# A differential-attention stage with its steps in another order on all engines

## The reference, cut to what matters

```python
h = rms_norm(x, norm1_g)
proj = h @ w_in                      # q, k: 4 heads x 2 components x 64; v: 4 x 128; xp: 4 groups x 128; gates
q = rms_norm(q, q_norm_g); k = rms_norm(k, k_norm_g)        # each over 64 channels
s = where(causal, (q @ k.T) * 64 ** -0.5, NEG_BIG)          # for both components c of a head
p = softmax(s)
a = (p[:, :, 0] - lam * p[:, :, 1]) @ v
a = rms_norm(a, subln_g) * (1 - lam_init)
...                                  # pooling branch, gates, w_up_attn, w_up_pool, w_o
u = square(relu(rms_norm(x) @ w_mlp_in)); x = x + u @ w_mlp_out
```

## Time and profile before

| what | value |
|---|---|
| time, median of 3 runs | 1289.74 us (1288.73 to 1290.46) |
| the profiled execution | 1288.65 us, its span 1286.8 us |
| TensorE busy | 1242.7 us, 97%, 6249 matmuls |
| VectorE busy | 960.5 us, 75%, 1450 |
| ScalarE busy | 562.1 us, 44%, 989 |
| GpSimd busy | 140.5 us, 11%, 229 |
| DMA | 174.38 MB, 136 GB/s on average |

### The profile page before, as it was taken

How to read it: one execution, slowest core, us unless ns; L and a number is a source line. 1 busy time by engine, 2 the same in 40 slices (tenths; PEclk the granted TensorE clock), 3 DMA queues, 4 the chain that set the end, 5 groups by cost and what they waited for, 6 DMA issues and landing times. The chain is left out here.

```text
span 1286.8 us, 17813 instructions
## 1 busy us (share of the span) xinstructions
PE 1242.7 (97%) x6249; PEld 1040.2 (81%) x6249; DVE 960.5 (75%) x1450; ACT 562.1 (44%) x989; POOL 140.5 (11%) x229
## 2 busy tenths in 40 slices
PE   4999898989999999999999999999999999999998
PEld 4878787878888888888888888888888878888887
DVE  4557777777898669783577877777778898979864
ACT  4446665665554322331344554453453423333330
POOL 2122323232200004000000000000000000000035
PEclk9999999999999999999999999999999999999999
DMA  8230202030246464632222445345459735253323
GB/s 275 89 115 2 83 1 81 0 98 17 83 156 207 143 205 153 226 129 99 99 82 93 167 150 172 137 142 172 151 181 349 284 126 202 98 206 121 96 96 135
DMA packets 113466, 174.38 MB, mean 136 GB/s; under 512 B 5469, under 2 KB 59378, under 8 KB 112882
## 3 DMA queue, kind: packets, MB, share of 16 engines
q1 hardware_dynamic: 113394, 173.44, 39.6%
HBM read 120.99 MB, written 52.43 MB: 135 GB/s over the span
## 5 line engine op out<-in xcount | busy, mean ns | idle before, releaser
L2202 PE MATMUL bank<-o_hi,s_hi 128*128 128x512 f32 x448 | 174.4, 389 | 1.8 <-DVE s_lo L2055 1.8
L2202 PE MATMUL bank<-o_hi,s_lo 128*128 128x512 f32 x448 | 174.3, 389 | 0.0
L2202 PE MATMUL bank<-slot_hi,featT_hi 128*128 128x256 f32 (+1 forms) x320 | 102.8, 321 | 1.0 <-ACT qkv L959 1.0
L2111 DVE TENSOR_TENSOR c<-bank,c 128x512 f32<-128x512 f32 x112 | 75.6, 688 | 35.6 <-PE bank L2202 34.0
L2202 PE MATMUL bank<-featT_hi,pair_hi 128*128 128x512 f32 x256 | 99.8, 390 | 0.8 <-DVE c L2111 0.7
L2202 PEld LDWEIGHTS bank<-o_hi,s_hi 128*128 128x128 f32 x448 | 84.1, 188 | 19.8 <-DVE s_lo L2055 2.2
L2202 PE MATMUL bank<-featT_hi,pair_lo 128*128 128x512 f32 x256 | 99.6, 389 | 0.0
L2202 PE MATMUL bank<-featT_lo,pair_hi 128*128 128x512 f32 x256 | 99.6, 389 | 0.0
L2202 PE MATMUL bank<-o_lo,s_hi 128*128 128x512 f32 x256 | 99.6, 389 | 0.0
L2202 PEld LDWEIGHTS bank<-o_hi,s_lo 128*128 128x128 f32 x448 | 84.1, 188 | 17.2
L2202 PE MATMUL bank<-slot_hi,featT_lo 128*128 128x256 f32 (+1 forms) x320 | 97.0, 303 | 0.0
(11 more groups left out here) (258 smaller groups left out, 3243.2 us busy)
## 6 DMA issues: line engine op xcount, KB each, us to landing
s_raw<-u_store SPq DMA_DIRECT2D x28, 1024.0 KB, 5.6
pair_raw<-in_w_mlp_in SPq DMA_DIRECT2D x16, 1024.0 KB, 6.0
u_store<-s_tile SPq DMA_DIRECT2D x64, 256.0 KB, 2.2
o_raw<-in_w_mlp_out SPq DMA_DIRECT2D x16, 1024.0 KB, 8.3
u_store<-u_tile SPq DMA_DIRECT2D x48, 256.0 KB, 2.4
raw<-in_w_in SPq DMA_DIRECT2D x20, 512.0 KB, 7.0
gate_store<-out_tile SPq DMA_DIRECT2D x32, 256.0 KB, 2.1
gate_raw<-in_w_in SPq DMA_DIRECT2D x8, 1024.0 KB, 5.5
```

The costliest lines, as they stand in the source:

```text
L2111: nc.vector.tensor_tensor(out[:], psum, other[:], ALU.add).then_inc(up_sum, 1)
L2202: mm = nc.tensor.matmul(out, a, b, start=start and i == 0, stop=stop and i == len(steps) - 1)
```

## The change

- *First loads*: norm1_g is queued ahead of the first value weights. ScalarE rounds x block 0 one weight block earlier and squares x block 1 ahead of weight blocks 2 and 3; VectorE makes the rest of x block 0 one weight block earlier. TensorE transposes x block 1 in the middle of v_project(0), not ahead of it.
- *Order of the steps*: value products get lag 4 and the output lag 5, so the drain has 5 steps. TensorE's step is: half of the projection, scores, the other half, q/k transposes, transpose of attn_norm, [pool projection or project(h, 0)], value products, weight transposes to TB and to TA. The order on ScalarE, VectorE and GpSimd follows: VectorE begins with o_sum and the q/k normalisation, then w_tok, the weight rests, attn_norm, the two maxima, the q/k rests, take_attn, and the sum of squares last.
- *Mask*: two matmuls behind the scores, identity by mask, add the mask to the diagonal tile in the bank; VectorE's 64 additions are gone. Identity and mask are rounded once by ScalarE.
- *Drain*: late_weights(4) and keep_first(2) on ScalarE and c11_add(1) and side_add(4) on VectorE move from behind the drain into its step 3.

```diff
--- before.py
+++ after.py
...
+        ident_r = at("ident_r", 215, [P, P], F32R)
+        mask_r = at("mask_r", 215.5, [P, P], F32R)
...
-            return 4 if isinstance(h, int) and h == HEADS else T
+            return 5 if isinstance(h, int) and h == HEADS else T
...
             load_x(0)
+            sp.dma_start(g1_row[:], norm1_g.to_broadcast([P, D])).then_inc(g1_in, 16)
             load_v_w(0)
-            sp.dma_start(g1_row[:], norm1_g.to_broadcast([P, D])).then_inc(g1_in, 16)
             load_v_w(1)
             load_x(1)
...
-                    soft, ts, us, _ = lagged(h, s, 2)
-                    there, t, u, _ = lagged(h, s, 3)
-
-                    long_rows = soft and ts >= 3
-                    if soft and not long_rows:
-                        exponential(0, ts, us)
+                    there, t, u, _ = lagged(h, s, 4)
                     if there:
-                        act.wait_ge(tb_full, tb + 1)
+                        act.wait_ge(tb_full, tb)
...
+                    there, t, u, of = lagged(h, s, 5)
+                    if there and not (last and t == T - 1):
+                        take_attn(t, of, ta + 1)
+                        ta = ta + 1
+                    soft, ts, us, _ = lagged(h, s, 2)
+                    pools = s == POOL_STEP and s < steps(h)
+                    if soft:
+                        exponential(0, ts, us)
+                    if s == 0 and not first:
+                        take_projection(h, s)
+                        square_qk(h, s)
+                    if pools:
+                        if soft:
+                            exponential(1, ts, us)
+                        if first:
+                            act.wait_ge(h_ready, T)
+                        take_pool(BANK_USES * h + POOL_STEP + 2, GROUPS - 1 - h, 0)
                     if late:
                         late(s)
-                    there, t, u, _ = lagged(h, s, 3)
+                    there, t, u, _ = lagged(h, s, 4)
                     if there:
                         act.wait_ge(out_full, u + 1)
                         wait(act, out_free, u)
...
+                    if soft and not pools:
+                        exponential(1, ts, us)
...
             x_square(0)
             v_w_hi(0)
+            x_hi(0)
             v_w_hi(1)
-            x_hi(0)
+            x_square(1)
             v_w_hi(2)
             v_w_hi(3)
-            x_square(1)
             x_square(2)
+            act.wait_ge(const_ready, 2)
+            nc.scalar.activation(ident_r[:], ident[:], ACT.Copy)
+            nc.scalar.activation(mask_r[:], mask[:], ACT.Copy)
...
+                if s == 3:
+                    late_weights(4)
+                    keep_first(2)
             head(HEADS, middle, late, between)
-            late_weights(4)
-            keep_first(2)
...
-                            diagonal = bank[:, 2 * c + t // 4, t % 4 * P:(t % 4 + 1) * P]
-                            nc.vector.tensor_tensor(diagonal, diagonal, mask[:], ALU.add).then_inc(masked, 1)
-                            dve.wait_ge(masked, 2 * u + c + 1)
...
+                    there, t, u, _ = lagged(h, s, 5)
+                    if there:
+                        dve.wait_ge(out_part, u + 1)
+                        nc.vector.tensor_tensor(o_sum[t % 2][:], bank[:, OUT, 0:P], o_part[:], ALU.add).then_inc(out_free, 1)
+                    normalise_qk(h, s)
...
+                        if not first or t > 0:
+                            dve.wait_ge(tb_full, tb_uses)
+                            if t == 0 or t > 4:
+                                dve.wait_ge(ta_full, ta_uses)
                         nc.vector.scalar_tensor_tensor(w_tok[:, 0:n], prob[1][:, 0:n], coef, prob[0][:, 0:n],
                                                        ALU.mult, ALU.add).then_inc(w_tok_ready, 1)
-                    if s > 0 or first:
-                        sum_squares(h, s)
+                    there, t, u, _ = lagged(h, s, 4)
+                    if there:
+                        n = min(t + 1, 4)
...
+                    there, t, u, _ = lagged(h, s, 5)
+                    if there:
+                        dve.wait_ge(a_scaled, u + 1)
+                        nc.vector.tensor_scalar(attn_norm[t % 2][:], o_sum[t % 2][:], a_scale[t % 2], None,
+                                                ALU.mult).then_inc(a_normed, 1)
+                    there, t, u, _ = lagged(h, s, 2)
+                    for c in range(2):
+                        if there:
+                            n = (t + 1) * P
+                            dve.wait_ge(score_full, 2 * u + c + 1)
+                            nc.vector.tensor_reduce(neg_max[t % 2][:, c:c + 1],
+                                                    bank[:, 2 * c:2 * c + 2, :].rearrange("p a b -> p (a b)")[:, 0:n],
...
+                    tb_uses = tb_uses + lagged(h, s, 1)[0] + lagged(h, s, 3)[0]
+                    ta_uses = ta_uses + lagged(h, s, 5)[0] + (lagged(h, s, 3)[0] and lagged(h, s, 3)[1] >= 4)
+                    sum_squares(h, s)
+                    if middle:
+                        middle(s)
...
             x_norm(0)
             v_w_lo(0)
+            x_lo(0)
             v_w_lo(1)
-            x_lo(0)
             x_norm(1)
...
+                if s == 3:
+                    c11_add(1)
+                    side_add(4)
             head(HEADS, middle, between)
-            c11_add(1)
-            side_add(4)
...
+                            nc.tensor.matmul(bank[:, 2 * c + p0 // 512, 0:p1 - p0], a, b, start=i == 0,
+                                             stop=i == 2 and p1 < n)
+                for c in range(2):
+                    diagonal = bank[:, 2 * c + t // 4, t % 4 * P:(t % 4 + 1) * P]
+                    nc.tensor.matmul(diagonal, ident_r[:], mask_r[:], start=False, stop=True).then_inc(score_full, 1)
...
-                    second, third = (4, 4) if last and s > 0 else (3, 5)
-
-                    scores_first = projects and s in (1, POOL_STEP + 1)
-                    if scores_first:
-                        scores(h, s, tb)
-                    part(range(second))
-                    if not scores_first:
-                        scores(h, s, tb)
-                    there, t, u, _ = lagged(h, s, 3)
-                    if there:
-                        pe.wait_ge(w_tok_ready, u + 1)
-                        wait(pe, tb_free, tb)
-                        weights_transpose(t, 0).then_inc(tb_full, 1)
-                        tb = tb + 1
                     w_first, w_second = tb, ta
-                    part(range(second, third))
-                    if there and t >= 4:
-                        wait(pe, ta_free, ta)
-                        weights_transpose(t, 1).then_inc(ta_full, 1)
-                        ta = ta + 1
-                        w_second = ta
-                    part(range(third, 8))
-                    if last and s == steps(h) - 1:
-                        first_products(3, range(KD))
+                    qk_uses = tb if first and s < 4 else tb - 1
+                    part(range(4))
+                    scores(h, s, qk_uses)
+                    part(range(4, 8))
                     there, t, u, _ = lagged(h, s, 1)
                     if there:
                         pe.wait_ge(qk_normed, u + 1)
...
                         nc.tensor.transpose(bank[:, TB, P:2 * P], qk_norm[t % 2][:, P:2 * P],
                                             ident[:]).then_inc(tb_full, 1)
                         tb = tb + 1
-                    there, t, u, of = lagged(h, s, 3)
-                    if there:
-                        if t == 0:
...
                         pool_project(h, 0, range(8))
                     if s == 0 and not first and projects:
                         project(h, 0, range(8))
+                    there, t, u, of = lagged(h, s, 4)
+                    if there:
+                        if t == 0:
+                            pe.wait_ge(v_in, 16 * of + 16)
+                        wait(pe, out_free, u)
+                        pe.wait_ge(tb_free, w_first)
...
+                        mm.then_inc(out_full, 1)
+                    there, t, u, _ = lagged(h, s, 3)
+                    if there:
+                        pe.wait_ge(w_tok_ready, u + 1)
+                        wait(pe, tb_free, tb)
+                        weights_transpose(t, 0).then_inc(tb_full, 1)
+                        tb = tb + 1
+                        if t >= 4:
+                            wait(pe, ta_free, ta)
+                            weights_transpose(t, 1).then_inc(ta_full, 1)
+                            ta = ta + 1
...
             x_transpose(0)
             for t in range(T):
-                if t + 1 < T:
+                if t > 0 and t + 1 < T:
                     x_transpose(t + 1)
-                v_project(t)
+                v_project(t, range(4))
+                if t == 0:
+                    x_transpose(1)
```

(38 more changed lines are left out.)

107 lines of the change are left out of this document (39 added, 68 removed).

## The result

| kernel | median, us | against the kernel before (95% interval) |
|---|---|---|
| before | 1290.10 (1288.73 to 1291.09) | |
| after | 1305.34 (1305.15 to 1307.13) | 1.0122 (1.0104 to 1.0139) |

The change makes the kernel 15.2 us slower. The side was forecast (+5.1 us), the size was not: 1305.3 lies above the range, which ended at 1301. The profiled execution took 1305.45 us, 16.8 more than that of before. Its slices look like those of before, and that is the first thing to see: nothing in them tells of 1.2%.

The account below looks back on a forecast made before the run. TensorE, busy nearly the whole span, was taken as the bound, so only its waits and added work counted. Gains and costs in opening and attention stage summed to +5.1 us, giving a median of 1294.8 us, range 1284 to 1301.

Parts of the forecast that it names:

- The step on the last head: Drain: side_add(4) ahead of o_sum and attn_norm on VectorE makes TensorE wait for late_lo, +2.7 us (0 to 4.3).
- The mask term: Attention stage: 64 mask matmuls of 128 columns on TensorE, covered by nothing, +5.5 us (3.8 to 7.4).
- The step on fewer cuts of the projection: Attention stage: weight transposes no longer cut the projection; 20 cuts and 32 steps save 3.4 us.
- opening: Opening: earlier norm1_g and x normalisation bring x_transpose(2) from 26.03 to about 20.3, -5.7 us.
- waits that go: Attention stage: waits before q/k transposes (20.2 us), scores (2.6) and for the kept gate tile (1.0) vanish.
- bank TB: Attention stage: weight transposes wait until the q/k rests leave TB at T+2.25, sixteen waits, +20.5 us.
- projection bank: Attention stage: TensorE waits for copies out of bank PROJ between its users, +5.1 us.
- VectorE late (rounds, head 0): Attention steps 2 and 3: VectorE's normalisation, weight rests and attn_norm come late, +3.7 us; head 0's late norm, +0.5.
- the step on the value tile: Attention step 4: the next head's value load delays TensorE, but ends before the TB wait does; costs nothing.
- TB sooner: Attention stage: bank TB is free earlier than T+2.25; at T+1.6 the time is 1284.4 us; chance 0.22.
- the rival on the opening's clock: Opening: TensorE's clock stays low, +3.4 us, so 1298.2; chance 0.10.
- one rival alone (1300.8): Attention stage: VectorE late in every step, 0.3 us more on five uncovered steps of 4 heads, +6; chance 0.08.

Follow-up runs that it names:

- the run without the reload: Kernel after with the three loop loads of v_tok left out, so heads 1 to 3 use head 0's value tile: 1305.46 us.
- side_add(1) first: Kernel after with side_add(1) ahead of the rest of first weight 3 on VectorE in the drain: 1304.29 us.
- sum of squares early: Kernel after with the sum of squares ahead of the q/k rests on VectorE: 1309.27 us.
- attn_norm early: Kernel after with attn_norm ahead of the two weight rests on VectorE: 1312.41 us.
- pool weight later: Kernel after with the pool weight's split at the end of step 3 instead of step 2: 1304.32 us.
- weight transposes moved: Kernel after with the weight transposes moved from the step's end to behind three k blocks of the next step's projection: 1297.33 us.
- mask twice: Kernel after with each mask matmul done twice: 1310.71 us.
- mask back: Kernel after with the mask addition back on VectorE: 1310.15 us.

## Why the prediction was wrong

Two steps of the prediction failed and one term was mis-sized with them. The step on the last head put attn_norm in the drain at nothing, and the runs show 3.0 us of waiting and 1.7 us of half clock there. The mask term was 5.5 us and measured 8.9. The step on fewer cuts of the projection took off 3.4 us, of which 0.2 is found. Together they are 11.3 of the 11.7 us that the sum missed in the profiled executions. In the prediction's own steps:

| step | forecast, us | measured, us |
|---|---|---|
| opening | -5.7 | -5.1 in the trace, -6.3 by its own run |
| waits that go | -23.8 | -25.0 |
| fewer cuts | -3.4 | -0.2 (what is left of the stage when all other rows are taken off) |
| bank TB | +20.5 | +20.3 |
| projection bank | +5.1 | +6.3 |
| VectorE late (rounds, head 0) | +4.2 | +5.4 |
| late_lo | +2.7 | +2.6 |
| mask matmuls | +5.5 | +8.9 |
| attn_norm in the drain | 0 | +3.0 |
| half clock behind it | 0 | +1.7 |
| rest of the program | 0 | -0.8 |
| sum | +5.1 | +16.8 (the rows give 17.1, by rounding and the count) |

- *Right:* the main mechanism. The wait for bank TB, the biggest term, came out at its size and at T+2.17, and the run without the reload shows that it hides the load of v_tok, as the step on the value tile said; its 4.1 us (counted from start to start) are in the 20.3. late_lo and the waits that go came out as well. The rival *TB sooner* (1284.4) is shown wrong by the same rows. The opening's gain is close, but its path was another in this trace: x_transpose(2) came at 20.90 (forecast 20.3), because the lower clock held up x_transpose(1) and VectorE waited for it. With the clock up early it was VectorE's chain, at 19.80. So the rival on the opening's clock was there in part:

```profile
8.24 1.94 PE L2222 MATMUL bank<-ident,h_row 128*128 128x128 f32 x8 [8.24 <-DVE h_row L1423]
...
17.09 1.04 PE L2222 MATMUL bank<-ident,h_row 128*128 128x128 f32 x8
...
20.90 1.09 PE L2222 MATMUL bank<-ident,h_row 128*128 128x128 f32 x8
```

- *Fewer cuts (3.2 us off).* The step subtracted what the weight transposes' cuts cost and did not put the mask's in their place. From the last score matmul to the mask it is 0.25 us on average, as it was to the weight transposes, so the 0.06 us in each of 32 steps did not go. And the second projection matmul behind the mask starts 0.17 us after the first instead of 0.12, in 27 steps. That is 1.9 and 1.4 us, about the 3.2. What I had priced for the mask at the earlier trace rows as half a narrow and wide pair (0.115) is right for a matmul behind another mask (0.113), but the first costs 0.16. In 32 steps that makes the 3.4 us of the mask term. The two steps fail in the same place: the border between the mask and its neighbours was read from rows in which no such border stands.
- *The drain (4.7 us off).* The sum went through VectorE's order at the last step only. The step on the last head looks at side_add(4) and not at side_add(1), which stood one step earlier in both kernels; it became costly because attn_norm went behind w_tok and the weight rests and its transpose went ahead of the products. Nor was VectorE's new order gone through for attn_norm in the drain, as it was for steps 2 and 3 of the rounds. The clock was weighed for the opening and nowhere else.
- *The range.* Nearly every part that the sum left out or cut short was on the slow side, while the range's upper end came from one rival alone (1300.8). The sum of the upper ends of three terms (mask 7.4, VectorE 5.5, tail 4.3) would have given 1300.1, and the drain's attn_norm was in none of them.
- *What the sum could not see.* It took the three parts of the change as a whole. The runs show that two of them are gains (-6.3 and -1.8) and the new order with its drain a loss of 24. The waits that the new order was to take away (20.5 us at the q/k transposes) are for the most part no matter of order: with the mask off VectorE, 8.6 of them are left.

## What to carry to other kernels

Before steps are re-ordered so that a wait goes away, take the work from the engine that the wait hangs on: here 0.6 us a step off VectorE removed 10 us of waits, and a new order of all engines traded 25 us of waits for 37. When two users of one buffer alternate, the wait depends on the time from the end of one user's last reader to the next user; putting them close behind each other on TensorE, with a chain of 2.2 us between, made a wait in 16 of 32 steps, and moving one by 1.1 us removed nearly all of these waits. Half of their time came back, mostly in other waits and cuts: 8 of 16 us were gained. A software pipeline's drain needs its own walk through every queue, since there the fillers between the steps are others.

## What the hardware showed that I had not expected

- *The same idle time of TensorE may be followed by some 3.4 us at the lower clock, by twice that, or by none.* Nine traces have the wait of 2.5 us for late_lo. Behind it the granted clock was 0.50 to 0.54 in six (side_add(1) first, no reload, sum of squares early, attn_norm early, pool weight later, weight transposes moved) and 1.00 in three (after, mask twice, mask back). In the old order with the new opening and mask, a wait of 0.76 us and one of 1.32, 1.8 us apart, were enough for a granted clock of 0.50 from 147.6 to 148.9. The drain's wait of 2.8 us for attn_norm was followed by 3.4 us of it in three kernels (after, no reload, sum of squares early), by 6.8 in two (mask twice, mask back) and by none in one (pool weight later). By half of TensorE's busy time in them, 3.4 us at the lower clock cost an estimated 1.5 to 1.7 us. The Trainium skill (TensorE: Matmul & The Clock Gate, What's actually happening) says that the activity is looked at in a free-running rhythm that doesn't start with the kernel; by that the same gap may or may not count, and these traces agree: of nine equal waits six are followed by the fall. Whoever removes one idle time may find the clock's fall behind another.
- *A 128-column matmul into the score banks costs 0.113 us behind another of its kind* (mask done twice), against 0.115 for a wide and a narrow value product on average and 0.03 between the last transpose and a projection matmul. The Trainium skill (same page, Back-to-back issue gap) gives 81 ns for sustained matmuls of 128 columns. These traces don't agree for theirs: in a row they stand 0.113 us apart (mask) and 0.109 (transposes).
